# Attention heads in pairs: weighted V on the two column halves of the TensorE array, sparse-branch scores on its two row halves

## What is computed

```
for l in range(2):
    h = rms_norm(x) * (1 + scale1) + shift1
    proj = h @ w_in                              # q, k, v of three mixers, indexer, gate logits
    # A: 8 heads, q and k of 96 channels (64 + 32 rotary), v of 64, causal
    # B: 4 heads of 64 channels, causal, linear distance bias (MoBA; one block of 256 keys here)
    # C: 4 heads of 64 channels, top-64 keys per query picked by an indexer, distance bias (DSA)
    s = q @ k.T * scale + mask_or_bias           # per head, 256 x 256
    y = softmax(s) @ v                           # per head, 256 x 64
    x = x + gate1 * ((sum_i sigmoid(g_i) * (y_i @ w_br_i)) @ w_out)
    x = x + gate2 * swiglu(rms_norm(x) * (1 + scale2) + shift2)
```

## Time and profile before

| | |
|---|---|
| Time, median of 3 runs | 954.27 us (952.56 to 957.33) |
| Profiled execution, its own time | 953.66 us |
| Its span | 951.5 us |
| PE busy | 911.0 us (96%) |
| PEld busy | 780.0 us (82%) |
| DVE busy | 704.9 us (74%) |
| ACT busy | 498.6 us (52%) |
| Granted TensorE clock, mean | 0.994 |

### The profile page before, as it was taken

The page is one execution under the profiler, slowest core; times in us unless marked ns, Lnnn a source line. Parts: engine busy times, 40 slices in busy tenths (PEclk is TensorE's granted clock), DMA queues, the critical chain, the costliest instruction groups (busy, mean ns, idle before and its releaser), DMA issues.

```text
span 951.5 us, 12781 instructions
## 1 busy us (share of the span) xinstructions
PE 911.0 (96%) x5020; PEld 780.0 (82%) x5020; DVE 704.9 (74%) x1125; ACT 498.6 (52%) x718; POOL 30.0 (3%) x53
## 2 busy tenths in 40 slices
PE   8998988999999999999989999899999999999998
PEld 6787978977887888888868999798789778888886
DVE  5987889788698757676579967997867966575444
ACT  5554865546448444353474469465464664344441
POOL 1010000000000000000000100000000000000000
PEclk9999999999999999999999999999999999999999
DMA  9978623513734867777637973242245446554451
GB/s 380 408 293 374 241 92 131 222 45 133 293 115 168 295 235 259 276 270 282 240 133 297 402 264 133 89 182 85 71 155 218 177 177 224 218 179 183 168 177 45
DMA packets 29581, 198.12 MB, mean 208 GB/s; under 512 B 3281, under 2 KB 3793, under 8 KB 7506
## 3 DMA queue, kind: packets, MB, share of 16 engines
q1 hardware_dynamic: 23474, 155.22, 43.6%
q0 software_dynamic: 5760, 41.95, 11.5%
q10 hardware_dynamic: 288, 0.14, 0.1%
HBM read 196.24 MB, written 1.05 MB: 207 GB/s over the span
## 4 chain that ended last, share of the span: by engine, by line
PE 61%; DVE 24%; ACT 8%; issue 4%; DMA 3%; DVEq 0%; ACTq 0%
PE bank L571 13%; PE bank L573 13%; PE bank L572 13%; DVE w_lo L1329 7%; PE bank L532 5%; PE bank L534 4%; PE bank L533 4%; ACT w_hi L973 3%; DMA raw<-in_slabs_dram 2%; DVE score L1552 2%; DVE front L1336 2%; DVE acc L1643 2%; DVE score L1570 1%; PE bank L908 1%; ACT acc L1211 1%
## 5 line engine op out<-in xcount | busy, mean ns | idle before, releaser
L1329 DVE TENSOR_TENSOR w_lo<-raw,w_hi 128x2048 fp32r<-128x2048 f32 (+2 forms) x146 | 317.5, 2179 | 133.9 <-ACT w_hi L973 131.9
L973 ACT ACTIVATE w_hi<-raw 128x2048 fp32r<-128x2048 f32 (+2 forms) x146 | 263.7, 1808 | 148.5 <-PE bank L573 96.7
L571 PE MATMUL bank<-w_hi,h_hi 128*128 128x512 f32 x536 | 211.2, 394 | 8.2 <-DVE w_lo L1329 5.1
L573 PE MATMUL bank<-w_lo,h_hi 128*128 128x512 f32 x536 | 209.2, 390 | 0.0
L572 PE MATMUL bank<-w_hi,h_lo 128*128 128x512 f32 x536 | 208.9, 390 | 0.0
L571 PEld LDWEIGHTS bank<-w_hi,h_hi 128*128 128x128 f32 x536 | 100.6, 188 | 34.3 <-DVE w_lo L1329 7.7
L573 PEld LDWEIGHTS bank<-w_lo,h_hi 128*128 128x128 f32 x536 | 100.6, 188 | 21.4
L572 PEld LDWEIGHTS bank<-w_hi,h_lo 128*128 128x128 f32 x536 | 100.7, 188 | 20.2
L532 PE MATMUL bank<-h_hi,w_hi 128*128 128x256 f32 x384 | 112.6, 293 | 4.6 <-DVE w_lo L1329 4.6
L533 PE MATMUL bank<-h_lo,w_hi 128*128 128x256 f32 x384 | 109.8, 286 | 0.0
L534 PE MATMUL bank<-h_hi,w_lo 128*128 128x256 f32 x384 | 109.8, 286 | 0.0
(11 more groups left out here) (206 smaller groups left out, 1361.7 us busy)
## 6 DMA issues: line engine op xcount, KB each, us to landing
raw<-in_slabs_dram SPq DMA_DIRECT2D x124, 1024.0 KB, 4.8
front<-in_ada_dram POOLq DMA_DIRECT2D x29, 1024.0 KB, 5.7
acc<-in_ada_dram POOLq DMA_DIRECT2D x11, 1024.0 KB, 8.1
raw<-in_slabs_dram SPq DMA_DIRECT2D x16, 552.0 KB, 7.7
front<-in_ada_dram SPq DMA_DIRECT2D x5, 1024.0 KB, 10.6
raw<-in_slabs_dram SPq DMA_DIRECT2D x6, 768.0 KB, 5.0
proj<-in_ada_dram SPq DMA_DIRECT2D x2, 1024.0 KB, 8.3
x_t<-in_x_dram SPq DMA_DIRECT2D x2, 512.0 KB, 4.4
```

The source lines that it names most:

```text
L571: nc.tensor.matmul(o, hh, wh, start=first, stop=False)
L573: return nc.tensor.matmul(o, hh, wl, start=False, stop=final)
L973: nc.scalar.activation(w_hi[:, n % RING, 0:w], raw[:, n % RING, 0:w], ACT.Copy).then_inc(hi_ready.sem, 1)
L1329: nc.vector.tensor_tensor(w_lo[:, n % RING, 0:w], raw[:, n % RING, 0:w], w_hi[:, n % RING, 0:w], ALU.subtract).then_inc(lo_ready.sem, 1)
```

## The change

`weigh_v` handles a pair of heads at once and issues the two heads' matmuls alternately, the even head on columns 0 to 63 of the array and the odd one on columns 64 to 127. It runs at the even iterations from 4, where before each head had its own iteration. Scores of branches b and c are also issued for two heads at once (`scores_pair`): each uses only its own 64 partitions, so rows 0 to 63 or rows 64 to 127 of the array. Scores now rotate over three banks (4, 5, 1), and all gate slabs from number 8 on use bank 0, so the wait of `gate_slab` asks for one gate activation more (`g` in place of `g - 1`).

```diff
 def gate_bank(g):
-    return 7 - g if g < 2 else g % 3 if g < 6 else g % 2
+    return 7 - g if g < 2 else g % 3 if g < 6 else g % 2 if g < 8 else 0
+SC_BANKS = (4, 5, 1)
...
-                    pe.wait_ge(gate_out.sem, gate_out.at(l, g - 2 if g < 8 else g - 1))
+                    pe.wait_ge(gate_out.sem, gate_out.at(l, g - 2 if g < 8 else g))
...
                 def scores(n):
-                    if n >= 2:
-                        pe.wait_ge(ttr_done.sem, ttr_done.at(l, 2 * (n - 1)))
-                    b = bank[4 + n % 2]
+                    if n >= 3:
+                        pe.wait_ge(ttr_done.sem, ttr_done.at(l, 2 * (n - 2)))
+                    b = bank[SC_BANKS[n % 3]]
...
+                def scores_pair(n):
+                    kind, h = HEADS[n]
+                    if n >= 2:
+                        pe.wait_ge(ttr_done.sem, ttr_done.at(l, 2 * (n - 1)))
+                    if n == 2:
+                        pe.wait_ge(gate_out.sem, gate_out.at(l, 8))
+                    j = 0 if kind == "c" else 1
+                    q = pq_t[:, 2 * j + h // 2, :]
+                    at = [slice(HD * e, HD * (e + 1)) for e in range(2)]
+                    b = [bank[SC_BANKS[(n + e) % 3]] for e in range(2)]
+                    for e in range(2):
+                        nc.tensor.matmul(b[e][:, 0:P], q[at[e], 0:P], kz_t[at[e], 4 * j + h + e, 0:P], start=True, stop=True)
+                    for e in range(2):
+                        nc.tensor.matmul(b[e][:, P:P + T], q[at[e], P:T], kz_t[at[e], 4 * j + h + e, :], start=True,
+                                         stop=True).then_inc(scored.sem, 1)
...
-                def weigh_v(n):
+                def weigh_v(pair):
+                    if pair >= 2:
                         pe.wait_ge(y_lo_done.sem, y_lo_done.at(l, pair - 1))
-                    pe.wait_ge(pt_out.sem, pt_out.at(l, n + 1))
+                    pe.wait_ge(pt_out.sem, pt_out.at(l, 2 * pair + 2))
...
+                    for e in range(2):
+                        nc.tensor.matmul(y[HD * e:HD * (e + 1), 0:T], proj[:, 0, at[e]:at[e] + HD], pt_sb[e][:, 0:T],
+                                         start=True, stop=False, skip_group_check=True)
+                    for e in range(2):
+                        nc.tensor.matmul(y[HD * e:HD * (e + 1), P:T], proj[:, 1, at[e]:at[e] + HD],
+                                         pt_sb[e][:, T:T + P], start=False, stop=True,
+                                         skip_group_check=True).then_inc(pv_done.sem, 1)
...
-                scores(0)
+                scores_pair(0)
                 for n in range(NH + 3):
                     if n + 1 < NH:
-                        scores(n + 1)
+                        if HEADS[n + 1][0] == "a":
+                            scores(n + 1)
+                        elif n % 2:
+                            scores_pair(n + 1)
                     if 2 <= n <= NH + 1:
                         turn_p(n - 2)
-                    if n >= 3:
-                        weigh_v(n - 3)
+                    if n >= 4 and n % 2 == 0:
+                        weigh_v(n // 2 - 2)
```

More of the change, by code:

```diff
@@ L778, in scores @@
                     kind, h = HEADS[n]
[L779 to L783, removed]
+                    if n >= 3:
+                        pe.wait_ge(ttr_done.sem, ttr_done.at(l, 2 * (n - 2)))
+                    q, k = qk_t[0:A_QK, h, :], qk_t[0:A_QK, A_HEADS + h, :]
+                    b = bank[SC_BANKS[n % 3]]
+                    nc.tensor.matmul(b[:, 0:P], q[:, 0:P], k[:, 0:P], start=True, stop=True)
+                    nc.tensor.matmul(b[:, P:P + T], q[:, P:T], k[:, :], start=True, stop=True).then_inc(scored.sem, 1)
+                def scores_pair(n):
+                    kind, h = HEADS[n]
                     if n >= 2:
                         pe.wait_ge(ttr_done.sem, ttr_done.at(l, 2 * (n - 1)))
-                    b = bank[4 + n % 2]
-                    nc.tensor.matmul(b[:, 0:P], q[:, 0:P], k[:, 0:P], start=True, stop=True)
-                    nc.tensor.matmul(b[:, P:P + T], q[:, P:T], k[:, :], start=True, stop=True).then_inc(scored.sem, 1)
+                    if n == 2:
[9 more added lines that the diff above has]
+                                         stop=True).then_inc(scored.sem, 1)
                 def turn_p(n):
@@ L800, in turn_p @@
                     last.then_inc(p_tp.sem, 1)
-                def weigh_v(n):
[L803 to L806, removed]
-                        pe.wait_ge(y_lo_done.sem, y_lo_done.at(l, pair - 1))
-                    pe.wait_ge(pt_out.sem, pt_out.at(l, n + 1))
[L810 to L815, removed]
@@ L817, in _ @@
-                scores(0)
+                def weigh_v(pair):
+                    if pair >= 2:
+                        pe.wait_ge(y_lo_done.sem, y_lo_done.at(l, pair - 1))
+                    pe.wait_ge(pt_out.sem, pt_out.at(l, 2 * pair + 2))
+                    y = bank[2 + pair % 2]
+                    at = []
+                    for n in (2 * pair, 2 * pair + 1):
+                        kind, h = HEADS[n]
+                        at.append({"a": P * h + A_NOPE, "b": C_BV + HD * h, "c": C_CV + HD * h}[kind])
+                    for e in range(2):
[5 more added lines that the diff above has]
+                                         skip_group_check=True).then_inc(pv_done.sem, 1)
@@ L1642, in scores_max @@
                     for t, (c0, c1) in enumerate(((0, P), (P, P + T))):
-                        nc.vector.tensor_tensor_reduce(p_sb[n % 4][:, c0:c1], bank[4 + n % 2][:, c0:c1], mask[:, c0:c1],
+                        nc.vector.tensor_tensor_reduce(p_sb[n % 4][:, c0:c1], bank[SC_BANKS[n % 3]][:, c0:c1], mask[:, c0:c1],
                                                        1.0, NEG, ALU.add, ALU.max, rowmax[n % 2][:, t:t + 1])\
```

## The result

The changed kernel takes 956.5 us at the median of 20 runs (955.06 to 958.36), the kernel before 953.34 us in as many runs (950.99 to 957.33). The ratio is 1.0033, with an interval of 1.0025 to 1.0041: about 3.2 us slower, inside the 0.5% that I had called no change, and nearly 2 us more than the +1.3 that I had forecast.

A forecast was written before the change was run, and what follows sets the result against it. The prediction took the stage as bound by DVE waiting on ACT, with PE, though busy, awaited in only four places per layer. Layer 0 +1.1 and layer 1 +0.2 gave +1.3 on 953.66: 955.0 us, range 952.5 to 959.5.

The forecast's parts named there:

- rival "faster": PE truly limits the stage, so its savings of 6.1 us per layer come through: 941.5 us; chance 0.08.
- bound of 1.3 us for a PE that needs no time: Most that could be gained: 0.2 us at iteration 13 plus 0.9 at layer 1's end, some 1.3 in all.
- four places at which the prediction has others wait for PE: Per layer: head 0's scores, ACT's copy in iteration 13, the last turn and last weighing; only there can time move.
- 0.2 for the start: Stage start: head 0's scores come 0.2 us later (0 to 0.2) for the array's change of shape.
- the rival to which I gave 0.10: Both halves' records start together, a pair's matmuls take 0.65 us; sum 0.0, 953.7 us; chance 0.10.
- taking turns (0.25): The array halves do not overlap, so a pair's matmuls stay at 1.30 us; sum +4.3, 958.0 us; chance 0.25.
- open weight loads (0.12): Half-row matmuls expose weight loads, 0.10 us each, on top of halves not overlapping; sum +7.1, 960.8 us; chance 0.12.
- the walk of the order: Adding lateness through each layer's start, iterations 12 and 13, and end: +1.1 us in layer 0, +0.2 in layer 1.
- main line: Halves overlap partly: weighed pair 1.02 us, paired scores 0.87 + 0.25; sum +1.3, 955.0 us; chance 0.30.
- 0.22 + 0.47: Lateness before iteration 13's turn: 0.22 us from weighing heads 8 and 9 together, 0.47 from scoring 14 and 15 together.
- Nearly all of it falls where nobody waits for PE: PE's weighing saving of 4.6 us per layer, and eight entries of 0.10, would hardly move the time.
- the cover of 0.9 us in iteration 10: Slack behind gate slab 10's longer wait, costed at nothing; lateness beyond 0.9 us would add one to one.

The follow-up runs named there:

- e4: Changed kernel plus unread filler matmuls in its longest PE gaps (iterations 5 and 10, and ahead of layer 0's last turn); ratio 1.0013 to the kernel before, +1.0 us.
- e1: Kernel before with only the weighing done in pairs; scores, banks and gate wait as before; ratio 1.0055 to the kernel before, +4.5 us.
- e2: Changed kernel with the old per-head weighing restored; paired scores, three banks and longer gate wait stay; ratio 1.0035 to the kernel before, +2.9 us.
- e8: Kernel before with only the last gate half moved from iteration 18 to 16; ratio 0.9985 to the kernel before, -1.3 us.
- e10: Changed kernel plus six unread filler matmuls ahead of layer 0's last turn alone; ratio 1.0022 to the kernel before, +2.8 us.

## Why the prediction was right or wrong

**Right: the bound.** PE's saving came, and came to nothing. The chain's share of PE fell from 61% to 54%. The rival "faster" is excluded by the stages, which are longer with 5 to 7 us less of PE. Its bound of 1.3 us for a PE that needs no time was too low, though: it left out head 0's scores and the 1.91 us behind the last turn, two of the four places at which the prediction has others wait for PE.

**Mis-sized: the prices of a pair.** I took 1.02 for a weighed pair, it is 0.80; 1.12 for a pair of scores with both changes of shape, it is 0.94 (0.86, and 0.08 ahead of it, by which the gate half of iteration 12 is longer: 231.38 - 228.32 = 3.06 for 2.98); 0.2 for the start, and the first `scores_max`, which stands 0.85 behind the first scores in the earlier trace rows, now stands 0.95 behind: 0.1. The step that failed is "PE starts records in order, so the other head's first record can only run beside this head's second". The records of both halves start together, as the rival to which I gave 0.10 had it; taking turns (0.25) and open weight loads (0.12) did not occur. That rival's prices give +0.45 in layer 0 and -0.46 in layer 1, and e4, the changed kernel with its clock kept, shows +0.65 and -0.28. With these prices the walk of the order was good to 0.2 us a layer; with the main line's it was not (+1.1 and +0.2).

**The signs.** The walk said that DVE would wait longer for `y_hi` at n = 13. It does, 1.72 in place of 1.28 (1.29 in layer 1), and so does e4 at its full clock; that is 0.44 where I had 0.22 + 0.47.

```profile
233.62 0.42 DVE L1690 TENSOR_TENSOR y_lo<-bank,y_hi 128x256 fp32r<-128x256 f32 x1 [1.72 <-ACT y_hi L1252]
```

It also said that the waits at the other odd n stay as they are. They do, but for n = 11 in layer 0 and n = 9 in layer 1, both behind a stretch at half clock, and for n = 17 and the last one at layer 1's end.

**Wrong: "Nearly all of it falls where nobody waits for PE", and so costs nothing.** What PE saves there becomes idle time, 12.5 us in place of 5.5 in layer 0's stage, and behind the long gaps PE ran at half its clock. That is most of the result: some 2.75 of 3.1 us by e4's stages, 0.0020 of 0.0033 by its time. Neither a term of my sum nor a rival had it. I had read the clock of 1.00 in the earlier trace rows as a property of the stage, when it went with the work that kept PE busy: take the single weighings away (e1) and it falls, put them back (e2) or fill the gaps (e4) and it stays up.

**Used up: the cover of 0.9 us in iteration 10.** I expected the gate half to end near 224.6. It started at 221.02, about as foreseen, but took 4.42 us in place of 2.98 and ended at 225.44, in a stage that had begun 0.6 earlier. That is some 1.4 us late against a cover of 0.9, and DVE's wait in iteration 11 grew by 0.60. I had written that beyond the cover it goes one to one; it did, and I had the condition but not what would meet it.

**The end.** From the last turn to the next dense matmul I had 1.91 + 0.22; it took 246.41 - 243.72 = 2.69, since weighing ran at half clock, and some 0.7 more went to slow dense matmuls behind it, which I hadn't at all. In layer 1 DVE's lead absorbed most of the lateness, as predicted: counted from the start of the stage, DVE is done with head 15 1.29 us later than before (707.05 + 0.55 against 703.33), and its turn starts only 0.38 later (707.65 against 704.29).

That the time lay near the forecast was in part luck: the order cost some 0.9 us less than I said, and the clock, which I had at nothing, some 2.75 more.

## What to carry to other kernels

Before TensorE is made faster in a stage that it does not bound, look at what will stand in the time saved. If nothing does, the granted clock may fall, and work of another stage or of the path behind the gap pays for it; move useful work into the gap (here a gate half, from +3.1 to -3.1 us in the stages with two small groups of fillers; the kernel before gains 1.7 by the same move, in e8), or leave the slow form. And the profile's clock by stretch is worth reading before and after each such change, since a busy share alone shows a saving where the time is lost.

## What the hardware showed

- Plain float32 matmuls of two records each, on the two column halves, run fully side by side: 0.80 us for two heads as for one, and 0.81 when one head's two matmuls are written ahead of the other's. On the two row halves a pair takes 0.86, where one head's took 0.65.
- Stretches at half clock (0.50 to 0.52) stood behind gaps of 1.7 to 2.8 us on PE, amid sparse work; the gap of 1.4 in the kernel before had none behind it. But the same gap of 2.4 was followed by one in layer 0 and not in layer 1, where one came behind a wait of 1.18, and the same program in layer 1 was at half clock about twice as long in e10 as in the kernel after. A gate half costs 2.98 us at one level and 4.42 when mostly at the other. Three groups of fillers, 14 matmuls in layer 0 and 8 in layer 1, made the kernel some 1.9 us faster.
